# A hybrid encoder layer with a two-level router: the router's products taken from the residual rows, and the slot matrices made by operations over several tiles

## The reference

```python
x = x + token_mixer(rms_norm(x, norm_mix[l]), ...)
hn = rms_norm(x, norm_ffn[l])       # y = x * rsqrt(mean(x*x) + EPS), times the vector g
x = x + hier_moe(hn, ...)
...
g_logits = xt @ w_rg + b_rg         # 4 groups: the largest is taken
e_logits = xt @ w_re + b_re         # 32 experts: the best 2 of the 8 in the group
g_idx = argmax(g_logits); top_v, top_i = top_k(e_sel, 2)
top_w = softmax(top_v) * softmax(g_logits)[g_idx]
...
h = silu(xt @ w_gate) * (xt @ w_up)           # per expert, D_EXPERT = 256
out = out + (h * combine) @ w_down
```

## Time and profile before

| | us |
|---|---|
| median of 3 runs | 632.04 (631.16 to 632.7) |
| the profiled execution, device time | 630.43 |
| its span in the profile | 628.4 |
| PE busy | 585.1 (93% of the span) |
| DVE busy | 269.8 (43%) |
| ACT busy | 210.7 (34%) |
| POOL busy | 80.9 (13%) |

### The profile page before, as it was taken

The page is one execution under the profiler, slowest core; times in us unless marked ns, Lnnn a source line. Parts: engine busy times, 40 slices in busy tenths (PEclk is TensorE's granted clock), DMA queues, the critical chain, the costliest instruction groups (busy, mean ns, idle before and its releaser), DMA issues.

```text
span 628.4 us, 8692 instructions
## 1 busy us (share of the span) xinstructions
PE 585.1 (93%) x3451; PEld 441.3 (70%) x3454; DVE 269.8 (43%) x582; ACT 210.7 (34%) x408; POOL 80.9 (13%) x112
## 2 busy tenths in 40 slices
PE   3999999999999999999999999999999998777894
PEld 3789979788577888888888874766666665443552
DVE  3647478645324368433362278411211211111447
ACT  3445456554486641432252241111111111011113
POOL 4000044000001100300000022112211221110001
PEclk9999999999998999999999999999999999998998
DMA  7476030902213122258879369799999999999994
GB/s 249 91 260 195 4 111 1 334 2 68 67 34 92 43 68 68 67 195 286 297 295 404 131 221 383 275 396 425 421 424 424 423 423 426 422 427 426 422 423 198
DMA packets 58281, 155.83 MB, mean 248 GB/s; under 512 B 8172, under 2 KB 38148, under 8 KB 45952
## 3 DMA queue, kind: packets, MB, share of 16 engines
q1 hardware_dynamic: 53392, 145.73, 60.4%
q0 software_dynamic: 4720, 9.45, 4.0%
q10 hardware_dynamic: 128, 0.09, 0.0%
HBM read 147.37 MB, written 15.75 MB: 260 GB/s over the span
## 4 chain that ended last, share of the span: by engine, by line
PE 66%; DMA 12%; DVE 7%; SPq 5%; issue 4%; ACT 3%; POOL 1%; DVEq 0%; POOLq 0%; ACTq 0%
PE bank L734 34%; PE bank L1124 13%; PE bank L1145 6%; PE bank L727 5%; DMA slot2a<-expert_w_up 5%; SPq L491 3%; DMA zt<-expert_rows 2%; DMA w<-w_in 2%; DMA expert_rows<-y,zcol 1%; PE bank L829 1%; SPq L444 1%; DMA x_in<-x 1%; PE bank L910 1%; DVE w_low L1637 1%; PE bank L933 1%
## 5 line engine op out<-in xcount | busy, mean ns | idle before, releaser
L1124 PE MATMUL bank<-slots,xgT 128*64 128x256 f32 x544 | 78.2, 384 | 4.9 <-DMA slot2b<-expert_w_up 2.5
L1719 DVE TENSOR_TENSOR w_low<-w,w_high 128x1024 fp32r<-128x1024 f32 x32 | 39.2, 1225 | 80.6 <-ACT w_high L1374 80.6
L1124 PEld LDWEIGHTS bank<-slots,xgT 128*64 128x64 f32 x544 | 52.5, 138 | 23.0 <-issue 4.3
L734 PE MATMUL bank<-x_high,w_high 128*128 128x512 f32 x168 | 67.0, 399 | 1.0 <-DVE x_low L1646 1.0
L734 PE MATMUL bank<-x_high,w_low 128*128 128x512 f32 x168 | 65.7, 391 | 0.0
L734 PE MATMUL bank<-x_low,w_high 128*128 128x512 f32 x168 | 65.6, 390 | 0.0
L1374 ACT ACTIVATE w_high<-w 128x1024 fp32r<-128x1024 f32 x32 | 33.7, 1054 | 49.1 <-PE bank L734 49.1
L2007 DVE TENSOR_SCALAR y<-bank,slot_weights 128x512 f32<-128x512 f32 x14 | 10.5, 751 | 89.9 <-PE bank L1145 89.9
L734 PE MATMUL bank<-w_high,x_high 128*128 128x420 f32 x128 | 45.4, 354 | 0.1
L734 PE MATMUL bank<-w_high,x_low 128*128 128x420 f32 x128 | 45.2, 353 | 0.0
L734 PE MATMUL bank<-w_low,x_high 128*128 128x420 f32 x128 | 45.2, 353 | 0.0
(11 more groups left out here) (279 smaller groups left out, 1168.3 us busy)
## 6 DMA issues: line engine op xcount, KB each, us to landing
slots<-expert_w_gate SPq DMA_DIRECT2D x19, 1024.0 KB, 27.8
slots<-expert_w_up SPq DMA_DIRECT2D x17, 1024.0 KB
slots<-expert_w_down SPq DMA_DIRECT2D x16, 1024.0 KB, 28.4
slot2b<-expert_w_down SPq DMA_DIRECT2D x9, 1024.0 KB, 8.4
w<-w_in SPq DMA_DIRECT2D x16, 512.0 KB, 3.7
slot2b<-expert_w_up SPq DMA_DIRECT2D x8, 1024.0 KB
slot2b<-expert_w_gate SPq DMA_DIRECT2D x8, 1024.0 KB, 19.0
w<-w_in SPq DMA_DIRECT2D x8, 840.0 KB, 4.8
```

Of the source, the lines that this page charges most:

```text
L734: ins_ = mm(out_, stat[a_], mov[b_], start=first and q_ == 0, stop=last and q_ == 2)
L1124: ins = mm(bank[2][e * SLOTS:(e + 1) * SLOTS, m * FE:(m + 1) * FE], xgT[:, c, e * SLOTS:(e + 1) * SLOTS], gu[m][e][:, c], start=(c == 0), ...
L1719: V.tensor_tensor(wl2[:, u % 2, :], raw2[:, u % 2, :], wh2[:, u % 2, :].bitcast(F32), ALU.subtract).then_inc(s["lo_done"], 1)
```

## The change

- The transposes, now `turn_x2(t)`, take the residual rows `x2[t]` and not the normed ones; all four tiles are turned before the first `route`.
- The vector `norm_ffn` is multiplied into the router's weights `rw` (one DVE operation in `gate_weights`, long before), for which it is loaded, transposed and copied beside `norm_mix` at the start of the program (one more DMA in ACT's queue).
- `router_out` multiplies by the root and adds the biases in one operation, one for each tile (4 in place of 2).
- `normed(2)` and `normed(3)` move behind `router_in`, and ACT's `row_squares(3)` behind the four `turned_rows`.
- `selb` is made from the sum of the two choices and comes before the two `sel`.
- `first_in` is made by two operations over all 8 `k`, and `hot[k, 0]` by three over 4, 3 and 1 of them, in place of 16 operations. Their source is a copy of `iota` in another order, made once by a DVE copy after `beforeb` (over the constant `before`, which nobody reads then).
- PE's `keep_busy` products: 19 for 22 ahead of the ranks, and none between the eight first-token products.

```diff
-            for t in range(3):
-                turn_hn(t)
+            for t in range(NT):
+                turn_x2(t)
             route(0, 2)
-            turn_hn(3)
+            route(2, 3)
             token_major(0, 2, 1)
-            route(2, 3)
             route(3, 4)
             token_major(2, 3, 2)
             token_major(3, 4, 3)
...
-            keep_busy(22)
+            keep_busy(19)
             pe.wait_ge(s["selb_done"], 1)
...
             for k in range(2 * NT):
-                pe.wait_ge(s["hot_done"], k + 1)
+                pe.wait_ge(s["hot_done"], 1 + sum(k >= k0 for k0 in HOT_CUTS[:-1]))
                 ins = mm(bank[6][:, 0:2], hot[:, k, 0, :], first_in[:, k, :], start=(k == 0), stop=(k == 2 * NT - 1))
-                if k < 2 * NT - 1:
-                    keep_busy(1)
             ins.then_inc(s["first_done"], 1)
...
-            act.dma_start(g8, norm_mix.rearrange("(c p) -> c p", p=P)).then_inc(s["norm_in"], 16)
+            for half_, gains in enumerate((norm_mix, norm_ffn)):
+                act.dma_start(g16[half_ * KC:(half_ + 1) * KC, :], gains.rearrange("(c p) -> c p", p=P)).then_inc(s["norm_in"], 16)
...
             for t in range(3):
                 row_squares(t)
-            turned_rows(0)
+            for t in range(NT):
+                turned_rows(t)
             row_squares(3)
-            turned_rows(1)
-            turned_rows(2)
             turned_logits(0, 2, 1)
-            turned_rows(3)
-            turned_logits(2, 3, 3)
+            turned_logits(2, 3, 2)
             turned_logits(3, 4, 4)
...
+            dve.wait_ge(s["cb_done"], 4)
+            dealt = K["before"]
+            V.tensor_copy(dealt.rearrange("p (x e l) -> p x e l", l=4, e=8), K["iota"].rearrange("p (x l e) -> p x e l", l=4, e=8)
+                          ).then_inc(s["cb_done"], 1)
...
+                V.tensor_tensor(rw[:], rw[:], bc(gcol_ffn, NG + EXPERTS), ALU.mult).then_inc(s["cb_done"], 1)
...
-                V.tensor_tensor(lg[:, t0:t1, :], bank[1 + t0][:, t0 * (NG + EXPERTS):t1 * (NG + EXPERTS)].rearrange(
-                    "p (t n) -> p t n", n=NG + EXPERTS), rb[:].unsqueeze(1).to_broadcast([P, t1 - t0, NG + EXPERTS]), ALU.add
-                    ).then_inc(s["rl_out"], 1)
+                for t in range(t0, t1):
+                    V.scalar_tensor_tensor(out=lg[:, t, :], in0=bank[1 + t0][:, t * (NG + EXPERTS):(t + 1) * (NG + EXPERTS)],
+                                           scalar=rstd2[:, t:t + 1], in1=rb[:], op0=ALU.mult, op1=ALU.add).then_inc(s["rl_out"], 1)
...
+            link(V.tensor_tensor(tmp8, hot1, hot2, ALU.add))
+            by_group = "p t (g i) -> p t g i"
+            V.tensor_tensor(selb[:].rearrange(by_group, g=NG), bc(g_hot, NE), tmp8.unsqueeze(2).to_broadcast([P, NT, NG, NE]),
+                            ALU.mult).then_inc(s["selb_done"], 1)
             for k, oh in enumerate((hot1, hot2)):
...
             link(ins)
-            V.tensor_tensor(selb[:], sel[:, 0], sel[:, 1], ALU.add).then_inc(s["selb_done"], 1)
...
-            for k in range(2 * NT):
-                V.tensor_scalar(hot[:, k, 0, :].rearrange("p (x e l) -> p x e l", l=4, e=8), dealt, pf[:, 0, k:k + 1], None, ALU.is_equal)
-                V.tensor_scalar(first_in[:, k, :], K["iota"][:, 0:2], pf[:, 1, k:k + 1], K["tokval"][:, k % NT:k % NT + 1],
-                                ALU.is_equal, ALU.mult).then_inc(s["hot_done"], 1)
+            link(V.tensor_tensor(first_in, K["iota"][:, 0:2].unsqueeze(1).to_broadcast([P, 2 * NT, 2]), bc(pf[:, 1, :], 2), ALU.is_equal))
+            first_by_way = first_in.rearrange("p (w t) i -> p w t i", w=2)
+            V.tensor_tensor(first_by_way, first_by_way.bitcast(F32), bc(K["tokval"][:, 0:NT], 2).unsqueeze(1).to_broadcast([P, 2, NT, 2]),
+                            ALU.mult)
+            for k0, k1 in zip((0,) + HOT_CUTS, HOT_CUTS):
+                V.tensor_tensor(hot[:, k0:k1, 0, :], dealt.unsqueeze(1).to_broadcast([P, k1 - k0, P]), bc(pf[:, 0, k0:k1], P),
+                                ALU.is_equal).then_inc(s["hot_done"], 1)
```

More of the change, by code:

```diff
@@ L131, in hybrid_encoder @@
         gn = sb("gn", [P, GV])
-        gcol = sb("gcol", [P, KC])
+        gcols = sb("gcols", [P, 2 * KC])
+        gcol, gcol_ffn = gcols[:, 0:KC], gcols[:, KC:2 * KC]
         row_norms = sb("row_norms", [P, 6, NT])
@@ L204, in hybrid_encoder @@
         relb, vrow = startup[0:BKT, 1700:1700 + HEADS], startup[0:HEADS, 1024:1536]
-        g8 = startup[0:KC, 1536:1536 + P]
+        g16 = startup[0:2 * KC, 1536:1536 + P]
         at_ = REST
@@ L286, in hybrid_encoder @@
         ZERO_PIECES = 2 * NT
+        HOT_CUTS = (4, 7, 8)
         arrived = {(n_, m_): sum(32 if q_ in HALVED else 16 for q_, (p_, w_, _) in enumerate(order)
@@ L738, in _ @@
             pe.wait_ge(s["ident_in"], 16)
-            pe.wait_ge(s["norm_in"], 16)
-            tr(bank[KC - 1][:, 0:KC], g8).then_inc(s["gc_done"], 1)
+            pe.wait_ge(s["norm_in"], 32)
+            tr(bank[KC - 1][:, 0:2 * KC], g16).then_inc(s["gc_done"], 1)
             for t in range(NT):
@@ L1028, in _, with turn_x2 @@
                 project(k, KC - 1).then_inc(s["wo_done"], 1)
-            def turn_hn(t):
-                pe.wait_ge(s["hn_done"], t + 1)
+            def turn_x2(t):
+                pe.wait_ge(s["x2_done"], 2 * (t + 1))
                 for c in range(KC):
-                    ins = tr(bank[2 * t + c // 4][:, (c % 4) * P:(c % 4 + 1) * P], hn_st[:, t, c * P:(c + 1) * P])
+                    ins = tr(bank[2 * t + c // 4][:, (c % 4) * P:(c % 4 + 1) * P], x2[:, t, c * P:(c + 1) * P])
                     if c % 4 == 3:
@@ L1037, in route @@
             def route(t0, t1):
+                pe.wait_ge(s["cb_done"], 7)
                 pe.wait_ge(s["hnT_outA"], t1)
@@ L1289, in _ @@
             act.wait_ge(s["gc_done"], 1)
-            A(gcol[:], bank[KC - 1][:, 0:KC], ACT.Copy).then_inc(s["gcol_done"], 1)
+            A(gcols[:], bank[KC - 1][:, 0:2 * KC], ACT.Copy).then_inc(s["gcol_done"], 1)
             def split_high(k):
@@ L1917, in _ @@
             residual(3)
-            normed(2)
             router_in(0)
             router_in(1)
-            normed(3)
+            normed(2)
             router_in(2)
             router_in(3)
-            router_out(0, 2, 2)
+            normed(3)
+            router_out(0, 2, 3)
             router_out(2, 4, 6)
-            dve.wait_ge(s["rl_out"], 2)
+            dve.wait_ge(s["rl_out"], NT)
             g_lg = lg[:, :, 0:NG]
@@ L1952, in _ @@
             V.tensor_tensor(ex, v2, v1, ALU.subtract).then_inc(s["rexp_in"], 1)
+            link(V.tensor_tensor(tmp8, hot1, hot2, ALU.add))
+            by_group = "p t (g i) -> p t g i"
+            V.tensor_tensor(selb[:].rearrange(by_group, g=NG), bc(g_hot, NE), tmp8.unsqueeze(2).to_broadcast([P, NT, NG, NE]),
+                            ALU.mult).then_inc(s["selb_done"], 1)
             for k, oh in enumerate((hot1, hot2)):
-                ins = V.tensor_tensor(sel[:, k].rearrange("p t (g i) -> p t g i", g=NG), bc(g_hot, NE),
+                ins = V.tensor_tensor(sel[:, k].rearrange(by_group, g=NG), bc(g_hot, NE),
                                       oh.unsqueeze(2).to_broadcast([P, NT, NG, NE]), ALU.mult)
             link(ins)
-            V.tensor_tensor(selb[:], sel[:, 0], sel[:, 1], ALU.add).then_inc(s["selb_done"], 1)
             dve.wait_ge(s["rank_done"], 1)
```

8 lines of the change are left out of this document (2 added, 6 removed).

## The result

| | before | after |
|---|---|---|
| median, us (9 runs each) | 632.70 (630.23 to 634.32) | 638.64 (634.95 to 640.31) |
| ratio after/before | | 1.0098, 95% interval 1.0076 to 1.0121 |
| profiled execution, us | 630.43 | 639.12 |
| its span | 628.4 | 637.1 |

The account below looks back on a forecast made before the run. The weights' stream, restarted by the first gather's landing, was taken as the bound; 2.8 us won ahead of the gather, cut to 1.6 at its landing, gave 628.8 against the profiled 630.4, so a median of 630.4, range 628.8 to 632.1 us.

Parts of the forecast that it names:

- The sum up to `gcolm`: PE and DVE work ahead of the first gather: gains of 0.8, 0.3 and 1.7 us, together 2.8 (1.7 to 3.0).
- Route: PE's transposes and routes up to the logits: transposes without a gap let the last `router_out` start earlier, gaining 0.8 us.
- Choice: DVE from logits to `selb`: two `sel` leave the way, one small operation comes in, gaining 0.3 us (0 to 0.3).
- Slot matrices: DVE's 16 operations merged and PE's eight products, up to `gcolm`: gain 1.7 us (1.0 to 1.9).
- I see no gap in the stream and the same end, 391.1 to 391.5: First loads around the gather: despite a later last store, they end as before, so the landing gains 1.6 us.
- Slower, 7%: Rival, 7%: loads run until 394, the gather takes its loaded 8.1 us and lands 1.9 later; 633.9 us.
- Edits at nothing: Edits priced at zero: `norm_ffn` DMA and transposition, DVE's copy and product on `rw`, PE without `keep_busy`.
- PE without the fillers: PE before the first gather's transposes: no cost, though its gap grows from nothing to about 1.5 us.
- the stream has a fixed number of bytes: From about 398 us on, the end is set by the weights' stream, which moves a fixed amount.
- one us at the gather's landing is one us at the end: Second part of the kernel: an earlier first landing passes fully to the end while the stream stays full.

Follow-up runs that it names:

- e2_norms: The changed kernel with the last squares and last two norms at their old places in ScalarE's and VectorE's lists; 635.25 us, ratio 1.0066.
- e11_late: e8_all with the last two norms and the last squares late, as in the changed kernel; ratio 1.0015.
- e8_all: e6_addresses with the last two norms and last squares at their old places and more filler products than the kernel before; ratio 0.9998.
- e6_addresses: The changed kernel with all SBUF addresses as before, the two vectors kept in a table unused then; ratio 1.0006.
- e1_busy: The changed kernel with PE's filler products as before (22 ahead of the ranks, one between the first-token products); 637.31 us, ratio 1.0080.
- e5_off32: The kernel before with only `gcol` 8 columns wider, so all tensors behind it start 32 bytes later; ratio 1.0060.
- e10_hold2: e8_all with the last two of the 21 first loads held until the first gather has landed; ratio 1.0005.
- e7_off64: The kernel before with only `gcol` 16 columns wider, so all tensors behind it start 64 bytes later; ratio 1.0057.
- e13_off128: The kernel before with only `gcol` 32 columns wider, so all tensors behind it start 128 bytes later; 634.58 us, ratio 1.0061.
- e9_hold1: e8_all with the last of 21 first loads held until the first gather has landed, and 9 fillers for 14 behind the tables; 630.12 us, ratio 0.9974.
- e4_slots: The kernel before with only the merged slot-matrix and first-token operations, and no filler between the eight products; 630.63 us, ratio 0.9983.
- e3_router: The changed kernel with the slot matrices and filler products as before, so the router part alone; 636.24 us, ratio 1.0068.
- e12_nofill: e8_all with the changed kernel's few filler products (19, 11, none, 7); ratio 0.9999.

## Why the prediction was wrong

The sum up to `gcolm` held. What failed is the end of the first loads, the clock behind the gather and, the largest part, the rate of the stream of weights.

**The terms ahead of the gather were right.** Route: from the first transpose to the end of the logits 9.20 for 9.94, 0.74 gained (0.8 forecast), and DVE waited for PE (1.33), not for the root, as worked out; the last norm, which did wait for it (0.80), ran in that gap. Choice: logits to `selb` 4.64 for 4.96, 0.32 gained (0.3). Slot matrices: 2.15 from the first operation to `gcolm` for 3.94, 1.79 gained (1.7). The three matrix operations, 1024 columns, took 1.35 end to end. The estimate by the formula of the Trainium skill (VectorE: DVE Perf Modes, section "The TRN2 errata — SBUF-src ops pay a fixed extra latency per instruction") was 1.54 for the three lengths added up, and my own from the rows, with neighbours overlapping, 1.27; the trace lies between, 0.19 under the page's figure. What I did not see: between `selb` and the matrices 3.22 passed for 2.89. POOL's zeroing of `xg` waits for the stores, so it moved from 379.57 to 382.96 and onto four of DVE's small integer operations. They took 0.61 to 0.42 where they took 0.17 before, and all ended when the zeroing did, at 384.8; that is 0.26 of the 0.33. Sum 2.52 for 2.8.

**The step "I see no gap in the stream and the same end, 391.1 to 391.5" failed.** The step reckoned only with what was left in the queue when the last store is issued. But the last load waits until that store has landed, and was issued at 382.93, 3.4 later than before; from 376 to 382 us 323 GB/s were moved for 401, and the engines were full until about 393.8. The gather was issued into this at 388.92 and landed at 396.67, from the stage's start 1.9 later than before. This is my rival "Slower, 7%", by its own condition (loads under way until 394) and its own price (landing 1.9 later; 8.1 forecast for the gather, 7.75 measured). Two pairs show that the late norm does it: after lands 2.3 later than e2_norms, and e11_late 1.5 later than e8_all. Not all of the 3.4 is the norm's: 0.7 is the later start, and in before that last store took 6.9 us to the last load, where it took 8.0 to 8.6 in the other kernels with early norms and nothing held back, so that e2_norms issued its last load only 1.5 earlier than after. More generally: in the nine kernels whose first gather took over 4 us, it landed 12.6 to 13.0 us behind the issue of the last load (13.7 in after), whether it was issued 6.0 behind that load (after, e6_addresses) or 8.4 (e8_all). So time won ahead of the gather was worth nothing unless the last load came earlier too. By the Trainium skill each DMA engine goes round its queues packet by packet (DMA: Bandwidth & Descriptors, section "Queues, rings and completion order"), and a gather would not stand behind all queued loads; 4.2 to 7.75 us with loads queued and 3.4 without speak against relying on that here.

**"Edits at nothing" failed twice.** PE without the fillers I put at nothing because the clock was 1.00 in all windows of before. The gap was not 1.5 but 2.91 us, and the granted clock behind it was 0.50: the eight transposes took 1.97 for 1.16, and landing to refill 5.67 for 3.51, 2.2 us. The fillers that were taken away are not enough to explain it, since e1_busy has them back and falls to 0.50 too; what after, e1_busy and e6_addresses share is the wait of about 3 us for a late gather. And the widening of `gcol` stood in no sum at all. It is the largest single part and the only one whose cost in time is clear of noise: +0.60% put into before (2.4 to 5.2 us), and 0.92% less when taken out of after. The step from "the stream has a fixed number of bytes" to an end that hangs only on the gather's landing took the stream's rate for granted; it was 416 to 418 GB/s for 423.

**What stays open.** The parts don't add up to a tenth of a per cent: after e5_off32's 0.60%, 0.38% are left for the middle of the kernel, which 2.4 to 4 us of later refill would explain; but e6_addresses has its refill 2.4 later than before and is within 0.0006 of it (interval up to 1.0031). At the old addresses the time doesn't follow the refill at all clearly: from the stage's start it came at 34.54 in e6_addresses, 32.80 in e11_late and 30.59 in e10_hold2, and the ratios are 1.0006, 1.0015 and 1.0005. So the prediction's rule that one us at the gather's landing is one us at the end is not borne out. Profiled executions of one kernel and the medians are not the same runs, and the intervals are 0.2% to each side. How much of a later refill reaches the end is therefore not settled better than "between none and all". Why the shift of the addresses changes the DMA rate is not known from these runs.

## What to carry to other kernels

When the end of a kernel is a saturated stream, compare the addresses of its buffers before anything else: here 32 bytes more in a small tensor allocated ahead of them cost more than the change could win. Time won ahead of a transfer counted here only if the transfers queued before it left earlier too; look for what the last of them waits for, and reckon the landing from there. And when a product's operand comes later, look at the clock in which its products will run, not only at the wait.

## What the runs showed of the hardware

- Loads of weights moved 422 to 424 GB/s with the ring at 48640 bytes of SBUF, and 416 to 420 with it and all tensors behind `gcol` 32, 64 or 128 bytes further on, the DMA engines full in both cases; the kernel before took 0.6% longer by such a shift alone (e5_off32, e7_off64, e13_off128). Window 480 to 520 of e13_off128:

```profile
480.00:520.00 40.00, 40.00 (x300) 26.57 (x298) 6.58 (x12) 5.18 (x10) 7.51 (x13) 1.00 1.02 419
```

- The first gather of rows took 3.4 us where the loads had run out or almost so (before, e5_off32, e9_hold1), and 4.2 (e8_all), 4.9 (e4_slots), 5.5 (e2_norms), 5.8 (e11_late), 6.0 (e1_busy), 6.9 (e6_addresses) and 7.75 us (after) with loads still under way.
- Four DVE operations, each on 8 integers and a constant, took 0.17 us each alone. Issued while POOL wrote zeros they all lasted until the zeroing ended: 0.61 to 0.42 in after, and 1.42 to 1.22 in e3_router, where they began 0.5 behind the zeroing's start. Two DVE operations on float32 that ran beside the zeroing in after kept their length (0.42 each, L1963 and L1965).
- Behind a wait of PE of 2.76 to 3.70 us (e1_busy, after, e6_addresses) the clock fell to 1.2 GHz for some 3 to 7 us, in e6_addresses only after the eight transposes. Behind a wait of 1.07 us (e11_late) it stayed at 2.4 GHz. The falls near 389 and 390 in after, e4_slots and e12_nofill came behind waits of 0.5 to 1.0 us between short products.
